# Gated linear attention with the tokens on the partitions: chunks in pairs, v projected straight into token order, squares on ScalarE

## The reference, cut to what matters

```python
q_in = qc * jnp.exp(bcum)
k_in = kc * jnp.exp(-bcum)
attn = jnp.where(tri, jnp.einsum('bhnik,bhnjk->bhnij', q_in, k_in), 0.0)
intra = jnp.einsum('bhnij,bhnjv->bhniv', attn, vc)
k_out = kc * jnp.exp(btot[:, :, :, None, :] - bcum)
dS = jnp.einsum('bhnjk,bhnjv->bhnkv', k_out, vc)
def step(S, inp):
    dec, ds = inp
    return S * dec[..., None] + ds, S
...
o = intra + inter          # inter = q_in @ S_start, per chunk
o = o * lax.rsqrt(jnp.mean(jnp.square(o), -1, keepdims=True) + RMS_EPS) * p['gla_norm_g']
y_b = o * jax.nn.silu(gg)  # then y_b @ p_b
```

## Time and profile before

| | |
|---|---|
| median of 3 runs | 1517.42 us (1510.96 to 1519.28) |
| span of the profiled execution | 1523.0 us |
| TensorE busy | 1262.4 us, 83% of the span |
| VectorE / ScalarE / GpSimd busy | 413.6 / 307.3 / 127.0 us |
| moved by DMA | 307.24 MB |

### The profile page before, as it was taken

One profiled execution on the slowest core, in us unless ns is written; L12 is line 12 of the kernel. 1 busy time (PEld: TensorE's weight loads), 2 busy tenths in 40 slices (PEclk: granted clock), 3 DMA queues, 4 the chain that ended last, 5 costly groups with the idle time before them and its releaser, 6 DMA issues.

```text
span 1523.0 us, 18481 instructions
## 1 busy us (share of the span) xinstructions
PE 1262.4 (83%) x6402; PEld 815.4 (54%) x6403; DVE 413.6 (27%) x704; ACT 307.3 (20%) x433; POOL 127.0 (8%) x203
## 2 busy tenths in 40 slices
PE   3899999999999999999987379798887977788710
PEld 3687878787878888888643223233332332233300
DVE  3326240423332260010386601111111111111156
ACT  3255550410000320000100012121211111111221
POOL 0100000000000000000000111111111111111134
PEclk9899999998878999999998579999998999889965
DMA  8744412124232213413003457996999999999631
GB/s 286 238 171 157 176 56 69 48 72 151 83 110 70 84 56 114 165 56 111 31 15 155 193 194 299 389 348 262 396 397 379 393 367 394 383 378 391 259 119 55
DMA packets 69930, 307.24 MB, mean 202 GB/s; under 512 B 10039, under 2 KB 18744, under 8 KB 56917
## 3 DMA queue, kind: packets, MB, share of 16 engines
q1 hardware_dynamic: 59786, 294.77, 50.5%
q0 software_dynamic: 6272, 10.14, 2.1%
q10 hardware_dynamic: 3820, 1.60, 0.4%
HBM read 298.35 MB, written 18.55 MB: 208 GB/s over the span
## 4 chain that ended last, share of the span: by engine, by line
PE 64%; DMA 18%; DVE 8%; issue 4%; ACT 3%; SPq 2%; ACTq 0%; POOL 0%; POOLq 0%; DVEq 0%; PEldq 0%
PE ps L1482 33%; DMA mem<-in_we_up 13%; PE ps L1750 12%; PE ps L1759 5%; PE ps L1709 3%; DMA mem<-in_w_mod 2%; PE ps L1639 2%; PE ps L1742 2%; PE ps L1636 1%; PE ps L1621 1%; DVE mem L1445 1%; PE ps L1647 1%; DMA mem<-in_we_gate 1%; DVE mem L1444 1%; PE ps L1515 1%
## 5 line engine op out<-in xcount | busy, mean ns | idle before, releaser
L1482 PE MATMUL ps<-mem 128*128 128x260 f32 (+1 forms) x2336 | 546.6, 396 | 10.3 <-ACT mem L813 3.9
L1482 PEld LDWEIGHTS ps<-mem 128*128 128x128 f32 (+1 forms) x2336 | 454.5, 196 | 95.3 <-issue 12.6
L1750 PE MATMUL ps<-mem 128*64 128x512 f32 x1120 | 286.7, 671 | 99.9 <-DMA mem<-in_we_up 78.4
L1750 PEld LDWEIGHTS ps<-mem 128*64 128x64 f32 x1120 | 89.7, 154 | 270.9 <-issue 270.9
L1424 DVE TENSOR_TENSOR mem<-mem,ps 64x512 f32<-64x512 f32 x35 | 24.1, 690 | 431.3 <-ACT mem L1002 431.3
L1759 PE MATMUL ps<-mem 128*64 128x512 f32 x560 | 129.2, 604 | 3.4 <-issue 3.4
L1002 ACT ACT_TABLE_LOAD x35 | 44.9, 1283 | 372.5 <-PE ps L1750 372.5
L1759 PEld LDWEIGHTS ps<-mem 128*64 128x64 f32 x560 | 37.5, 138 | 66.8 <-issue 64.5
L710 POOL DMA_INDIRECT pair_scratch<-mem x35 | 32.7, 934 | 458.2 <-DVE mem L1416 458.2
L1416 DVE COPY mem<-ps 64x512 f32<-64x512 f32 x70 | 48.1, 688 | 78.1 <-PE ps L1759 77.0
L1709 PE MATMUL ps<-mem 128*128 128x512 f32 x128 | 59.8, 628 | 0.0
(11 more groups left out here) (284 smaller groups left out, 988.7 us busy)
## 6 DMA issues: line engine op xcount, KB each, us to landing
mem<-in_we_gate SPq DMA_DIRECT2D x32, 2048.0 KB, 12.0
mem<-in_we_up SPq DMA_DIRECT2D x32, 2048.0 KB, 16.5
mem<-in_we_down SPq DMA_DIRECT2D x32, 2048.0 KB, 8.9
mem<-in_w_in SPq DMA_DIRECT2D x14, 2048.0 KB, 8.5
mem<-in_w_mod SPq DMA_DIRECT2D x12, 2048.0 KB, 12.0
out<-mem SPq DMA_DIRECT2D x13, 512.0 KB, 5.3
mem<-in_state_gla SPq DMA_DIRECT2D x8, 512.0 KB, 3.9
mem<-v_scratch SPq DMA_DIRECT2D x8, 512.0 KB, 4.3
```

Of the source, the lines that this page charges most:

```text
L1482: ins = pe.matmul(out[0:m, h, 0:HALF], w[:, k, col:col + m], src[:, k, h * HALF:(h + 1) * HALF], start=(k == 0), stop=(k == KD - 1))
L1750: ins = pe.matmul(ps[CAP * q:CAP * q + CAP, 2 + j, :], xT[j][:, k, :], ring[3 * slot + q][:, k, :], start=(k == 0), stop=(k == KD - 1))
```

## The change

v is projected with the tokens on the output partitions: `hT` becomes the stationary side and the weights the moving side, 512 columns wide. The 8 sample rows are projected apart in four column quarters (`vs`). The transpositions of v are gone; the bias is added by DVE from a copy spread over the partitions.

The loop runs over 4 pairs of chunks. The scores of a pair are one 128x128 block per head. `ds` of the two chunks uses the two row halves of the array; `o` comes out with tokens on the partitions, the two chunks in the two column halves, 256 values wide; the eight products of the samples' states (`sample_out`) run in four column quarters with 8 stationary columns. The sum of squares leaves TensorE: ACT squares `o` out of PSUM with an accumulator (`square`), takes the root, and DVE scales (`normal`), all inside the loop. The normed result is turned by TensorE between the blocks of ga (`turn`) and multiplied with the gate by DVE.

```diff
-    for c in range(8):
-        jobs.append(("v", c))
-        if c:
-            jobs.append(("vt", c - 1))
-    jobs.append(("vt", 7))
+    for g in range(2):
+        jobs += [("v", 2 * g), ("v", 2 * g + 1), ("vs", g)]
-    for n in range(NCH):
-        jobs += [("ds", n), ("gg", n), ("os", n)]
+    for p in range(PAIRS_OF_CHUNKS):
+        jobs += [("ds", 2 * p), ("ds", 2 * p + 1), ("gg", 2 * p), ("o", p), ("gg", 2 * p + 1)]
-        jobs += [("ga", c), ("ss", c)]
-    jobs += [("pa", c) for c in range(4)]
+        jobs += [("ga", c), ("ot", c)]
+    jobs += [("ot", 4)] + [("pa", c) for c in range(4)]
...
+            def copy_v(n):
+                await_job(sc, ("v", n))
+                g, i = n // 2, 2 * (n % 2)
+                sc.activation(v_tok[:, i:i + 2, g * 512:(g + 1) * 512], slot_banks(("v", n)), ACT.Copy)\
+                  .then_inc(freed(("v", n)), 1)
...
+            def square(p):
+                r = rows(p)
+                for h in range(HEADS):
+                    cols = slice(h * DVH, (h + 1) * DVH)
+                    if p < 4:
+                        src, out = slot_banks(("o", p))[:, h // 2, (h % 2) * DVH:(h % 2 + 1) * DVH], o_tok[:, p, cols]
+                    else:
+                        src, out = o_samp[0:r, cols], squares_out[0:r, :]
+                    ins = sc.activation(out, src, ACT.Square, accum_out=ss[0:r, p, h:h + 1])
+                    if p < 4:
+                        ins.then_inc(sq_ready, 1)
+                    else:
+                        link(ins)
+                if p == 4:
+                    sc.sem_inc(sq_ready, HEADS)
+            def root(p):
+                sc.wait_ge(var_ready, p + 1)
+                sc.activation(rms[0:rows(p), p, :], ss[0:rows(p), p, :], ACT.Sqrt).then_inc(rms_ready, 1)
...
-            for n in range(NCH):
-                gate(n)
-                await_job(sc, ("os", n))
-                sc.activation(O[:, :, T + n:T + n + 1], slot_banks(("os", n))[:, 0, 0:8].unsqueeze(2), ACT.Copy)\
-                  .then_inc(freed(("os", n)), 1)
...
+            for p in range(PAIRS_OF_CHUNKS):
+                gate(2 * p)
+                await_job(sc, ("o", p))
+                square(p)
+                root(p)
+                gate(2 * p + 1)
+            sc.wait_ge(os_done, NS)
+            sc.wait_ge(st_ready, NS)
+            for h in range(HEADS):
+                link(sc.activation(o_samp[0:NS, h * DVH:(h + 1) * DVH], ps[32 * h:32 * h + NS, 7, 0:DVH], ACT.Copy))
+            sc.sem_inc(os_copied, 1)
+            square(4)
+            root(4)
...
+            v.wait_ge(bias_in, 16)
+            for n in range(4):
+                v.wait_ge(freed(("v", n)), INDEX[("v", n)] // 3 + 1)
+                g, i = n // 2, 2 * (n % 2)
+                vt = v_tok[:, i:i + 2, g * 512:(g + 1) * 512]
+                v.tensor_tensor(vt, vt, v_bias[:, g * 512:(g + 1) * 512].unsqueeze(1).to_broadcast([P, 2, 512]), ALU.add)\
+                 .then_inc(v_ready, 1)
...
+            def normal(p):
+                r = rows(p)
+                v.wait_ge(sq_ready, HEADS * (p + 1))
+                v.tensor_scalar(ss[0:r, p, :], ss[0:r, p, :], 1.0 / DVH, RMS_EPS, ALU.mult, ALU.add).then_inc(var_ready, 1)
+                v.wait_ge(rms_ready, p + 1)
+                link(v.reciprocal(rms[0:r, p, :], rms[0:r, p, :]))
+                for h in range(HEADS):
+                    cols = slice(h * DVH, (h + 1) * DVH)
+                    if p < 4:
+                        o, src = o_tok[:, p, cols], slot_banks(("o", p))[:, h // 2, (h % 2) * DVH:(h % 2 + 1) * DVH]
+                    else:
+                        o = src = o_samp[0:r, cols]
+                    link(v.scalar_tensor_tensor(o, src, rms[0:r, p, h:h + 1], norm_g[0:r, :], ALU.mult, ALU.mult))
+                if p < 4:
+                    v.sem_inc(freed(("o", p)), 1)
+                v.sem_inc(on_ready, 1)
+            v.wait_ge(norm_in, 16)
+            v.wait_ge(kt_ready, 1)
+            for p in range(PAIRS_OF_CHUNKS):
+                masked(p)
+                next_state(2 * p)
+                next_state(2 * p + 1)
+                sample_state(2 * p)
+                normal(p)
+                sample_state(2 * p + 1)
+            normal(4)
...
+            for g in range(2):
+                w = weight_tile()
+                for n in (2 * g, 2 * g + 1):
+                    out = start(("v", n))
+                    for b in range(2):
+                        i = 2 * (n % 2) + b
+                        for k in range(KD):
+                            ins = pe.matmul(out[:, b, :], hT[:, k, i * P:(i + 1) * P], w[:, k, :],
+                                            start=(k == 0), stop=(k == KD - 1))
+                    done(ins)
+                out = start(("vs", g))
+                for k in range(KD):
+                    for c in range(4):
+                        ins = pe.matmul(out[32 * c:32 * c + NS, 0, 0:P], hT[:, k, T:NT], w[:, k, c * P:(c + 1) * P],
+                                        start=(k == 0), stop=(k == KD - 1))
+                done(ins)
+                last_of_tile(("vs", g))
...
+            def sample_out(b):
+                pe.wait_ge(st_ready, b + 1)
                 for h in range(HEADS):
+                    ins = pe.matmul(ps[32 * h:32 * h + NS, 7, 0:DVH], q_diag[:, h, b * NS:(b + 1) * NS], st[b % 2][:, h, :],
+                                    start=(b == 0), stop=(b == NS - 1))
+                ins.then_inc(os_done, 1)
+            for p in range(PAIRS_OF_CHUNKS):
+                cols = slice(p * P, (p + 1) * P)
+                if p >= 1:
+                    pe.wait_ge(attm_ready, p)
+                for h in range(HEADS):
+                    ins = pe.matmul(ps[:, 6, h * P:(h + 1) * P], Q[:, HEADS + h, cols], Q[:, h, cols], start=True, stop=True)
                 ins.then_inc(at_done, 1)
+                ds = [start(("ds", 2 * p + q)) for q in range(2)]
                 for h in range(HEADS):
+                    for q in range(2):
+                        ins = pe.matmul(ds[q][:, h // 2, (h % 2) * DVH:(h % 2 + 1) * DVH],
+                                        kout_tok[64 * q:64 * q + 64, p, h * P:(h + 1) * P],
+                                        v_tok[64 * q:64 * q + 64, p, h * DVH:(h + 1) * DVH], start=True, stop=True)
+                        if h == HEADS - 1:
+                            done(ins)
+                if p % 2 == 0:
+                    w = weight_tile()
+                project(("gg", 2 * p), w, (2 * p % 4) * P, P, hT)
+                pe.wait_ge(attm_ready, p + 1)
+                pe.wait_ge(s_ready, 2 * p + 1)
+                out = start(("o", p))
+                for h in range(HEADS):
+                    o = out[:, h // 2, (h % 2) * DVH:(h % 2 + 1) * DVH]
+                    for q in range(2):
+                        ins = pe.matmul(o[64 * q:64 * q + 64, :], attm[p % 2][:, h, q * CH:(q + 1) * CH],
+                                        v_tok[:, p, h * DVH:(h + 1) * DVH], start=True, stop=(2 * p + q == 0))
+                    for q in range(2):
+                        n = 2 * p + q
+                        if n:
+                            ins = pe.matmul(o[64 * q:64 * q + 64, :], Q[:, h, n * CH:(n + 1) * CH], S[n % 3][:, h, :],
+                                            start=False, stop=True)
                 done(ins)
+                sample_out(2 * p)
+                project(("gg", 2 * p + 1), w, ((2 * p + 1) % 4) * P, P, hT)
+                if p % 2 == 1:
+                    last_of_tile(("gg", 2 * p + 1))
+                sample_out(2 * p + 1)
+            def turn(i):
+                pe.wait_ge(on_ready, i + 1)
+                r = rows(i)
+                src = o_tok[:, i, :] if i < 4 else o_samp[0:r, :]
+                out = start(("ot", i))
+                for k in range(KD):
+                    ins = pe.transpose(out[:, k // 4, (k % 4) * P:(k % 4) * P + r], src[:, k * P:(k + 1) * P], ident[0:r, 0:r])
```

More of the change, by code:

```diff
@@ L42 @@
 NCH = T // CH
+PAIRS_OF_CHUNKS = NCH // 2
 RANK = 16
@@ L241, in build @@
         upper = keep(P)
-        maskT = keep(CH)
+        maskT = keep(P)
+        q_diag = keep(HEADS, NS * NS)
+        norm_g = keep(DVH)
+        ss = keep(TILES, HEADS)
+        rms = keep(TILES, HEADS)
         sel8 = keep(P)
@@ L628, in _ @@
                                pattern=[[0, P]], channel_multiplier=1))
[L629 to L632, removed]
+            link(pool.affine_select(out=maskT[:], in_=maskT[:], compare_op=ALU.is_ge, fill=0.0, base=0,
+                               pattern=[[1, P]], channel_multiplier=-1))
+            link(pool.memset(maskT[0:CH, CH:P], 0.0))
+            link(pool.memset(q_diag[:], 0.0))
             pool.sem_inc(consts, 1)
@@ L646, in _ @@
             pool.sem_inc(consts, 1)
-            pool.wait_ge(yb_ready, KD)
+            pool.wait_ge(yb_ready, TILES)
+            for j in range(2):
+                pool.wait_ge(st_out[j], 16 * (NS // 2))
```

(35 more changed lines are left out.)

218 lines of the change are left out of this document (76 added, 142 removed).

## The result

The changed kernel takes 1443.67 us (median of 4 runs, 1439.76 to 1444.49) against 1517.14 before: ratio 0.951, 95% interval 0.948 to 0.954. The forecast was 1444.

A forecast was written before the change was run, and what follows sets the result against it. TensorE was taken to bound v, the chunk loop and ga; gains of 1.6 + 69.8 + 1.7 = 73.1 us took the median from 1517.4 to 1444 us, range 1433 to 1466.

The forecast's parts named there:

- The bound: v, chunk loop and ga: TensorE (PE) is busy nearly throughout (65.5, 164.5, 35.2 us), so shortening its work shortens the kernel.
- Stage of v: Projection of v: 55.9 us of products, 1.6 start, 3.6 sample rows, 4.4 tail; sum 65.5, a gain of 1.6.
- the tail: From v's last product to the first scores: samples' copies, bias and turn of k, left at 4.4 us (3.5 to 6).
- A pair: Two chunks in the loop: 22.4 us of PE work, 1.4 wait and 0.4 clock make 24.2; loop gain 69.8.
- The wait: PE's second `sample_out` waits for DVE behind `normal`: a 9.2 us chain against 7.7 of PE work, 1.4 a pair.
- The rival of emptying PSUM: Loop: squares cost twice a plain pass, PE waits 3.0 us a pair plus 2.1 at lower clock; 1457 us, chance 0.20.
- The forecast's own 0.4 us a pair for the clock behind the wait: Loop: allowance of 0.4 us a pair for PE running slower after a 1.4 us wait, judged from the experts' stage.
- before `o` ends DVE is on time: Loop: DVE's mask, two states and a sample make 9.0 us, against 2.4 + 7.3 + 3.65 of PE work.
- one of the prediction's own signs of being wrong: Loop: gap over 3 us, clock near 0.8, L1666 taking 4 us, or PE waiting elsewhere, above all for a sample's v.
- ga: Stage after the loop: four sums of squares (6.1 us) give way to five groups of transpositions (4.4 us); gain 1.7.
- the 0.18 us passes: Old loop's 64-column products for `o`, some 0.18 us a pass, said to pay for loading weights, not for columns.
- the forecast's price for 512 KB in any direction: Loop transfers on SP's queue: state out 5.3 us, state in 3.9, v 4.3, all expected hidden.

## Why the prediction was right

- **The bound.** PE in the loop, as read: what shortened its work shortened the kernel, and the gain reached the end. The three stages gave 75.0 us for a forecast of 73.1. That the median then came within 0.4 us of 1444 is partly luck, as the experts' stage alone differs by more than 5 us between two traces of the changed kernel.
- **Stage of v**, 65.5 forecast, 65.4 measured, by two errors that cancel. The start at the lower clock cost about 3.1 us, not 1.6 (30.77 for the first 64 passes against 27.70 for the second), and the tail was about 3, not 4.4.

```profile
276.43 30.77 PE L1629 MATMUL ps<-mem 128*128 128x512 f32 x64
...
309.39 27.70 PE L1629 MATMUL ps<-mem 128*128 128x512 f32 x64 [0.33 <-PE ps L1635]
```

- **A pair**, 24.2 forecast, 23.8 measured. Increments 1.93 for 2.4: the row halves run together fully. Scores 1.09 for 0.9, samples 1.1 for 0.9, output 3.6 for 3.65. PE's work was 22.2 for 22.4.
- **The wait**, 1.62 for 1.4: the chain took 9.4 for 9.2. A square with its accumulator cost what the lower bound said, since the read-out of 0.19 to 0.22 us lies under the next square. The rival of emptying PSUM had the right place, but its price was too high. The forecast's own 0.4 us a pair for the clock behind the wait falls out: nothing was lost behind 1.6 us. Those 0.4 us are what the pair came out shorter by, since the wait, priced 0.2 too low, and the work, 0.2 too high, cancel. Behind a wait of 3.7, 1.6 us were lost, not the 2.1 that the rival took from the earlier trace rows.
- **The first pair** waits elsewhere, which I had not seen: 1.49 us at the first sample. DVE stood 4.48 us at L1213 for the write of v to memory, because the third state buffer lies on the samples' v (`vs_out`). So the step "before `o` ends DVE is on time" failed in this pair, and one of the prediction's own signs of being wrong came: PE waiting elsewhere, for v of a sample. That this wait is about as long as those of the other pairs is chance, and it kept the sum right.

```profile
351.23 2.03 DVE L1213 SCALAR_TENSOR_TENSOR mem<-mem,ps 128x256 f32<-128x256 f32 x4 [4.48 <-DMA v_scratch<-mem]
...
357.21 0.62 PE L1652 MATMUL ps<-mem 128*8 128x256 f32 x8 [1.49 <-DVEq L1226]
```


- **ga**, 2.9 for 1.7: the turns cost 0.88 us start to start, as priced, but a gate block 7.0, not 7.28, so that the four sums of squares had cost 7.0 and not 6.1.
- **A step that failed, though no term rests on it.** I read the 0.18 us passes as the price of loading weights. The runs show the turn between 64 and 128 rows in its place. The forecast stood because each new product was priced by a row of its own kind, without turns. The lower clock that came with it was counted as gone, and was: 1.00 in the loop. Why turns and one-column passes bring the clock down stays open; the runs show only that it stays up without them.

By the experiments the loop's 70.4 us divide so: taking the turns out of the output, 27.7 (165.8 to 138.1); then the samples' thin products, 23.9 (to 114.2, with an eighth of them left); the rest, 18.8 (to 95.4), is left for the wider operands and the halves in parallel, less 6.4 us of new waits. The order of the steps matters, since the first two share the clock.

## What to carry to other kernels

Price a new product by a row of its own shape and tiling, and take products with different row counts out of each other's way before widening anything: here those turns alone cost 28 us. When work leaves TensorE for a chain through two other engines, add up that chain against what TensorE still has queued, and put whatever TensorE waits for ahead of it; here a wait of 1.6 us cost only itself, and one of 3.7 cost the clock as well. The clock can also be lost without a gap: before, PE was busy for 99% of the loop at a granted 0.81, with turns between row counts and one-column passes in it. So a busy engine at a granted 0.8 is worth a look.

## What the runs showed of the hardware

- A pass for the other half of the array starts beside passes that stand up to four places ahead of it: 16 passes in two blocks of eight took 2.89 us, eight of them in the middle 0.11 us apart and the others 0.22, where in turns they took 1.93.
- The write of 32 KB to memory between L1190 and L1213 kept DVE until 7.9 us after it was asked for, longer than the forecast's price for 512 KB in any direction. In the 4.2 us before it a load of 2 MB and two of 512 KB had been asked for on the same queue (7.9 and a median of 7.6 us to landing); no run has the write alone.
